# The last scaling of every second tile moved from VectorE to GpSimd, in a decoder layer on one core

## The reference, cut to what matters

```
x = x + m @ w_out
f = hier_moe(rmsnorm(x, ln2_g), ...)        # two experts per token, weighted
x = x + f
y = x * rsqrt(mean(x * x) + 1e-6) * final_g # final norm, output y
```

## Time and profile before

| what | us |
|---|---|
| median of three executions | 866.26 (863.41 to 869.72) |
| the profiled execution, its own time | 867.14 |
| span of the profiled execution, first to last instruction | 865.4 |
| TensorE busy in the span | 752.7 |
| VectorE busy in the span | 364.8 |
| ScalarE busy | 239.6 |
| GpSimd busy | 140.9 |
| tail, first addition to end of last scaling | 38.21 |

### The profile page before, as it was taken

One profiled execution on the slowest core, in us unless ns is written; L12 is line 12 of the kernel. 1 busy time (PEld: TensorE's weight loads), 2 busy tenths in 40 slices (PEclk: granted clock), 3 DMA queues, 4 the chain that ended last, 5 costly groups with the idle time before them and its releaser, 6 DMA issues.

```text
span 865.4 us, 11816 instructions
## 1 busy us (share of the span) xinstructions
PE 752.7 (87%) x4461; PEld 375.7 (43%) x4461; DVE 364.8 (42%) x1023; ACT 239.6 (28%) x556; POOL 140.9 (16%) x193
## 2 busy tenths in 40 slices
PE   6999999599999989899999259999999999999400
PEld 3666665256666645455555223333333333333100
DVE  0556665554458454565565711111111111111087
ACT  2766665400531534111111101111111111111022
POOL 1011001000121121021121221221122211221132
PEclk9999999698999989999999669999999999999855
DMA  9201200210110012611214648999999999992193
GB/s 335 103 25 49 105 7 1 101 53 0 55 37 19 1 48 92 279 73 51 95 50 172 266 115 294 416 395 420 409 404 417 405 420 406 399 376 96 65 388 142
DMA packets 28055, 164.10 MB, mean 190 GB/s; under 512 B 7017, under 2 KB 8193, under 8 KB 17738
## 3 DMA queue, kind: packets, MB, share of 16 engines
q1 hardware_dynamic: 19778, 145.34, 42.4%
q0 software_dynamic: 8080, 17.51, 5.5%
q10 hardware_dynamic: 144, 0.52, 0.2%
HBM read 151.14 MB, written 23.12 MB: 201 GB/s over the span
## 4 chain that ended last, share of the span: by engine, by line
PE 76%; DVE 10%; issue 5%; DMA 4%; ACT 4%; ACTq 0%; POOL 0%; DVEq 0%; SPq 0%; POOLq 0%
PE PS L1772 20%; PE PS L1788 10%; PE PS L1486 7%; PE PS L1623 6%; PE PS L1631 5%; PE PS L1607 4%; PE PS L1598 3%; PE PS L1487 3%; PE PS L1757 3%; PE PS L1515 2%; PE PS L1587 2%; PE PS L1669 2%; PE PS L1471 2%; DMA xin<-in_x 1%; DVE RA L1425 1%
## 5 line engine op out<-in xcount | busy, mean ns | idle before, releaser
L1772 PE MATMUL PS<-BIG,RD 128*32 128x512 f32 x1536 | 171.4, 598 | 0.0
L1772 PEld LDWEIGHTS PS<-BIG,RD 128*32 128x32 f32 x1536 | 47.9, 110 | 105.9 <-issue 105.9
L1788 PE MATMUL PS<-BIG,RD 128*32 128x512 f32 x768 | 87.3, 595 | 0.7 <-ACT RD L915 0.7
L1384 DVE SCALAR_TENSOR_TENSOR RD<-RD,PS 128x256 f32<-128x256 f32 x25 | 10.5, 421 | 177.4 <-ACT RD L898 177.4
L1486 PE MATMUL PS<-BIG,RA 128*128 128x512 f32 x128 | 66.7, 603 | 4.6 <-DMA BIG<-in_wqkv 3.1
L708 POOL DMA_INDIRECT ypair<-RD,pids x25 | 25.3, 1013 | 228.9 <-DVE RD L1400 219.0
L1631 PE MATMUL PS<-BIG 128*128 128x512 f32 x128 | 59.7, 612 | 0.0
L1607 PE MATMUL PS<-RA,BIG 128*128 128x344 f32 x192 | 58.7, 467 | 0.0
L1623 PE MATMUL PS<-BIG 128*128 128x512 f32 x128 | 58.2, 598 | 0.0
L1598 PE MATMUL PS<-RA,BIG 128*128 128x344 f32 x192 | 57.2, 453 | 0.0
L898 ACT ACTIVATE RD<-PS 128x256 f32<-128x256 f32 x25 | 9.6, 385 | 169.0 <-PE PS L1772 161.8
(11 more groups left out here) (265 smaller groups left out, 1024.4 us busy)
## 6 DMA issues: line engine op xcount, KB each, us to landing
BIG<-in_wexp SPq DMA_DIRECT2D x33, 2048.0 KB, 12.7
BIG<-in_wexp SPq DMA_DIRECT2D x33, 1024.0 KB, 13.1
xin<-in_x SPq DMA_DIRECT2D x16, 512.0 KB, 3.4
BIG<-ypair SPq DMA_DIRECT2D x8, 1024.0 KB, 8.6
BIG<-in_wxy SPq DMA_DIRECT2D x4, 1024.0 KB, 4.8
out_y<-RD SPq DMA_DIRECT2D x8, 512.0 KB, 4.2
xtab<-RD SPq DMA_DIRECT2D x7, 512.0 KB, 3.4
BIG<-in_wqkv SPq DMA_DIRECT2D x4, 768.0 KB, 10.1
```

Of the source, the lines that this page charges most:

```text
L1772: o = MM(PS[own, 2 + p2, :], xgT[:, p2, k, own], wgu[expert(n, j) % NG][:, k * 512:(k + 1) * 512], start=(k == 0), stop=(k == KD - 1))
L1788: o = MM(PS[own, 5 + half, :], hT[:, p2, k, own], wdn[expert(n, j) % ND][:, at:at + 512], start=(k == 0), stop=(k == KF - 1))
```

## The change

The scaling of tiles 0, 2, 4 and 6 is made by GpSimd, as a tensor_scalar by `rs3` into `ob[0]` and then a tensor_tensor by the gain in place. VectorE scales tiles 1, 3, 5, 7 and 8. The order on VectorE becomes: additions of tile t+1, mean of tile t, and, for even t from 2 on, the scaling of tile t-1; tile 8's scaling is last. Output buffer 0 belongs to even tiles, buffer 1 to odd ones, as before, and each now has a semaphore of its own (`ob_ok[0]`, `ob_ok[1]`). GpSimd's loop over tiles is written out instead of run as a hardware loop. The semaphore `x3a` between a tile's two additions gives way to `dve_done`.

```diff
-        ob_ok = sem("ob_ok")
+        ob_ok = [sem("ob_ok0"), sem("ob_ok1")]
-        x3a = sem("x3a")
 @@ SyncE
-                sp.wait_ge(ob_ok, t + 1)
+                sp.wait_ge(ob_ok[t % 2], t // 2 + 1)
 @@ GpSimd
-            with pool.Fori(0, NT) as t:
+            pool.wait_ge(gf_in, 16)
+            for t in range(NT):
                 pool.wait_ge(var3_ok, t + 1)
-                root(rs3[:, ds(t, 1)], ss3[:, ds(t, 1)], rs3_ok)
+                root(rs3[:, t:t + 1], ss3[:, t:t + 1], rs3_ok)
+                if t % 2 == 0 and t < NPT:
+                    pool.wait_ge(rs3_ok, t + 1)
+                    if t >= 2:
+                        pool.wait_ge(o_out[0], 16 * (t // 2))
+                    nc.gpsimd.tensor_scalar(ob[:, 0, :], x2_all[:, t, :], rs3[:, t:t + 1], None, ALU.mult).then_inc(pool_done, 1)
+                    pool.wait_ge(pool_done, 2 * NFT + t // 2 + 1)
+                    nc.gpsimd.tensor_tensor(ob[:, 0, :], ob[:, 0, :], gfb, ALU.mult).then_inc(ob_ok[0], 1)
 @@ VectorE
-                V.scalar_tensor_tensor(x2, yp[:, t % 4, 0:D_MODEL], comb[:, t, 0:1], x2, ALU.mult, ALU.add).then_inc(x3a, 1)
-                dve.wait_ge(x3a, t + 1)
+                V.scalar_tensor_tensor(x2, yp[:, t % 4, 0:D_MODEL], comb[:, t, 0:1], x2, ALU.mult, ALU.add).then_inc(dve_done, dq.up())
+                dve.wait_ge(dve_done, dq.now())
 ...
-                    .then_inc(ob_ok, 1)
+                    .then_inc(ob_ok[t % 2], 1)
 ...
             add_y(0)
-            mean(0)
             dve.wait_ge(gf_in, 16)
             for t in range(NT):
                 if t + 1 < NT:
                     add_y(t + 1)
-                finish(t)
-                if t + 1 < NT:
-                    mean(t + 1)
+                mean(t)
+                if t >= 1 and t % 2 == 0:
+                    finish(t - 1)
+            finish(NT - 1)
```

## The result

The changed kernel takes 874.22 us at the median of 20 runs, the kernel before 867.34 on the same chips: a ratio of 1.0082 with a 95% interval of 1.0062 to 1.0103, some 7 us slower. That is within the 1% forecast, on its slower side, with the upper end of the interval just over 1%. 871.5 had been forecast, which was +5.2 on the 866.26 of three executions; the twenty of each kernel give +6.9.

A forecast was written before the change was run, and what follows sets the result against it. VectorE was taken to bound the tail: 38.21 us would become 30.9 plus 11.4 to 13.6 of waiting for SBUF, so +4.1 to +6.3, middle +5.2. Set against the median 866.26, that gave 871.5 us, range 864 to 876.

The forecast's parts named there:

- the 42.3 to 44.5 that the sum gave: Tail, first addition to last scaling: 30.9 us without SBUF meetings plus 11.4 to 13.6 of VectorE waiting, against 38.21.
- the 42 to 44.5 named as a sign of being right: Tail: last scaling ends 42 to 44.5 us after the first addition if the engines take turns at SBUF.
- the 9.6 to 10.1: Tail: us that a pair of tiles would take, against 8.0 before.
- the closing: After the last scaling: 4.83 us of output and closing work, expected to stay as it was.
- The holding: Tail: VectorE waits nearly the whole time of eight GpSimd products for its turn at SBUF, 11.4 to 13.6 us.
- The first product: GpSimd's tensor_scalar in the tail: taken as 1.04 us at 1024 columns, from a row of 1032 columns at 1.05.
- waits for roots: Tail: last two scalings wait 0.7 us; one or two more may wait 0.4 to 0.6, inside the forecast's spread.
- Load 5: SyncE's queue: issued about 835.2, landing 843.7 after 8.5 us, wanted at 843.3; nothing counted for it.
- rival (c): Tail: load 5 and load 7 land late behind outputs GpSimd makes; slower by over 1%, 875.5 us; chance 0.15.
- (b): Tail: additions do not wait for a running GpSimd product; 863 us, down to 859; chance 0.14.
- (d): Tail: GpSimd's first tensor_scalar after the indirect transfers starts late; over 3.5 us of it passes 1%; chance 0.04.
- The order on VectorE: Tail: additions ahead of the previous tile's mean remove 1.35 us at the start and 0.13 in each of eight periods.

The follow-up runs named there:

- the idle-product kernel: Kernel before, with an unneeded two-input GpSimd product added behind the roots of tiles 0, 2, 4 and 6: stretch 43.7 us, ratio 1.0054.
- the pair with constants and fills: Changed kernel with four output and nine load buffers: constants in GpSimd's first product, stretch 41.2 us, ratio 1.0021; zero fills for both products, 34.0 us, 0.9922.
- The kernel with constants: Changed kernel, GpSimd's first product using constants 1.0 and 0.0 instead of the per-token root: stretch 42.4 us, ratio 1.0029.

## Why the prediction was right, and where its sizes were off

**The sign and the cause held; that the size did is in part luck.** GpSimd's products and VectorE's additions and scalings take turns at reading SBUF, in both orders; the idle-product kernel and the pair with constants and fills show it on this very instruction. That the loss stays under 1% of the time held too, at 0.82%. But the stretch, 46.8 us, lies above the 42.3 to 44.5 that the sum gave and above the 42 to 44.5 named as a sign of being right; of the three pairs from tile 2 to tile 8 two took 9.9 us, inside the 9.6 to 10.1, and the one with the late load 11.4. The terms below missed in both directions, and the closing, which the prediction took as fixed, hid another 1.6 us.

**The holding was mis-sized, 11.4 to 13.6 us against 5.9.** Two reasons. The first product holds VectorE for 0.7 us, not for its whole time; the step took its price from a copy that was held to the end by a two-input sum, and put it on a product with one tile as input as well. And a product holds nobody when VectorE is waiting for something else, as it did behind tile 0's second product, behind tile 2's first and at the end. The prediction counted tile 6's products whole in this term, though it knew that nothing runs beside them; what VectorE waited there, 2.2 us for the root behind them, is in the waits for roots below, and with it the term is at most 8.1. Where hardly anything else was waited for, the holding was 8.3 with the short form: some two thirds of the term.

**The first product was given 1.04 us and takes 2.7.** The row used was a product with constants; the one added has a number per partition. This did not hold VectorE, it delayed what stands behind: waits for roots of 5.7 us where the prediction had 0.7 and, inside its spread, one or two of 0.4 to 0.6. The kernel with constants is 4.4 us of stretch shorter, with 1.6 us of such waits.

**The output buffer was left out.** GpSimd waits for the output of tile t-2 before tile t, 0.8 to 2.1 us each, 3.9 in all; with four buffers the stretch is 4.2 shorter. The prediction followed SyncE's queue for the loads, and did not ask when the output that GpSimd itself has just finished late would land: it is issued at 835.02, and GpSimd could start on tile 2 at 838.08.

**Load 5** was issued at 835.40 (835.2 forecast; from the first addition, 13.7 us instead of 12.8) and landed in 6.5 us, faster than the 8.5 assumed, at 841.9. It was still late by 2.5, because VectorE was held less than forecast up to there and wanted it at 839.4, not at 843.3. This is rival (c)'s place with another cause: the load was not slow. The changed kernel's rows are the load's issue and landing and the addition that waited:

```profile
L577 SPq DMA_DIRECT2D BIG<-ypair x1: 431/431/431, 835.4 to 835.4; - x1
...
DMA to landing us min/median/max: 6.5/6.5/6.5
```

```profile
841.93 1.28 DVE L1430 SCALAR_TENSOR_TENSOR RA<-BIG,comb,RA 128x1024 f32<-128x1024 f32 x1 [2.52 <-DMA BIG<-ypair]
```

**Rivals (b) and (d)** fell. Additions do wait for a running product, though for the first one only 0.7 us. And GpSimd's first tensor_scalar started 0.10 after the root before it had ended (827.06 + 1.47 to 828.63), after the indirect transfers as before them:

```profile
827.06 1.47 POOL L612 TENSOR_TENSOR stat<-stat,mhalf 128x1 f32<-128x1 f32 x1 [10.32 <-DVE stat L1443]
828.63 3.50 POOL L744 TENSOR_SCALAR RD<-RA,stat 128x1024 f32<-128x1024 f32 x1
```

**The order on VectorE** was counted as 2.4 us of gain. Alone it leaves the stretch unchanged: the loads and an output buffer take the gain back, and only when those were widened did it show (38.2 to 34.6). The prediction also took ScalarE's 0.13 off every mean, but in the new order the mean of tile 8 has no additions ahead of it: 1.27 us of waiting in the changed kernel.

**The closing** was taken as fixed after the last scaling. While GpSimd works to the end it hangs on GpSimd's last instruction, here a root, and it fell by 1.6.

Together: held 5.9, roots 5.7 and the mean of tile 8 behind ScalarE 1.3, loads 3.0, the last output buffer 0.9, wide work 29.4, and means and small gaps 0.6 make 46.8, 8.6 over before; less 1.6 of closing and 0.7 of an earlier start is the span's +6.3, and the runs' medians say +6.9. Forecast was +5.2: one term twice too large and four too small or left out, which nearly cancelled. That the time came out near is owed to this as much as to the mechanism.

## What to carry to other kernels

Before moving a wide instruction from VectorE to GpSimd, see in the trace whether the instructions that stay on VectorE are longer beside GpSimd's reads, or GpSimd's beside them: here 1.28 us taken away per tile brought back up to 2.7 us of holding. Take the duration of a GpSimd instruction only from a row of the same form, number per partition or constant. And when an engine becomes the maker of an output, follow its own buffer's release and what the next loads stand behind, as for any other wait.

## What the runs showed that was not expected

- GpSimd's tensor_scalar of 128x1024 takes 2.71 us with a number per partition and 0.90 with constants, counted from the end of the addition before it; it holds a two-input instruction of VectorE that is ready in time for 0.74 to 0.86 in the first form and 0.66 to 0.78 in the second. The Trainium skill, "SBUF — State Buffer", section "Who interferes with whom", has a VectorE instruction with two SBUF inputs and a GpSimd instruction that reads SBUF block each other, the second to issue fully until the first finishes, and says that one which only writes it does not contend. The traces agree nearly for the two-input product (1.97 of 2.2) and agree for fills, which held nobody (1.28 throughout), but not for the form with a number per partition, where 0.74 of 2.71 was measured.
- By the Trainium skill, "GPSIMD Engine Reference", section "2.1 Instruction dispatch", the first call of a freshly loaded routine costs some 6 us more. The trace shows 0.10 between the root and the first tensor_scalar of the tail; no run shows whether a routine is loaded afresh there.
- A two-input product with both inputs the same tile held VectorE for 1.64, one with different inputs for 1.96 to 2.03 where VectorE was ready in time.
- In every kernel whose GpSimd worked to the end, the span ended 6.1 to 6.2 us after GpSimd's last instruction; without it, 2.2 after the last scaling. The time goes by in GpSimd's DRAIN; what it waits for was not tried.
